# Query-key dots in float32r over the full array instead of float32 pairs on half arrays

## The reference

```
D_MODEL, SEQ, DEC_SEQ, PAST_LEN, DEPTH = 1024, 1024, 64, 256, 2
# group A: 8 query heads on 2 key heads, dim 64; indexer: 4 heads, dim 64, one key
q_a, k_a, v_a, gate_a, q_i, k_i, w_i, q_b, k_b, v_b, gate_b = split_cols(h @ w_in)
q_a, k_a, q_i, k_i = rope(...)
rel   = relu(einsum('bqhd,bsd->bqhs', q_i, k_i))            # index dots
score = einsum('bqhs,bqh->bqs', rel, w_i) * IDX_SCALE        # then the top 256 keys of each query
logits = einsum('bqngd,bqknd->bqngk', q_a, chosen_keys) * HD ** -0.5     # attention dots
o_a = softmax(logits) @ chosen_values
o_b = retention(rope(q_b), rope(k_b), v_b, state)            # 4 heads, dim 128
mixed = concat(o_a * silu(gate_a), groupnorm(o_b) * silu(gate_b))
x = x + gate * rms_norm(mixed @ w_out)
```

## Time and profile before

| what | value |
|---|---|
| median of three runs | 1437.32 us |
| span of the profiled execution, first to last instruction | 1434.8 us |
| what the median has beyond that span | 2.5 us |
| mean granted clock of TensorE | 0.996 |
| TensorE busy | 1389.2 us (97%) |
| VectorE busy | 1008.5 us (70%) |
| ScalarE busy | 784.4 us (55%) |
| GpSimd busy | 405.2 us (28%) |
| layer 0: `idx` steps | 38.8 to 116.4 us |
| layer 0: `ret` and `gate` steps | to 421.5 us |
| layer 0: `att` steps | to 610.7 us |
| layer 0: `out` steps | to 747.2 us |
| layer 1: `att` steps | 1106.2 to 1295.2 us |

### The profile page before, as it was taken

How to read it: one execution, slowest core, us unless ns; L and a number is a source line. 1 busy time by engine, 2 the same in 40 slices (tenths; PEclk the granted TensorE clock), 3 DMA queues, 4 the chain that set the end, 5 groups by cost and what they waited for, 6 DMA issues and landing times.

```text
span 1434.8 us, 24595 instructions
## 1 busy us (share of the span) xinstructions
PE 1389.2 (97%) x7687; PEld 1065.3 (74%) x7687; DVE 1008.5 (70%) x2983; ACT 784.4 (55%) x1916; POOL 405.2 (28%) x382
## 2 busy tenths in 40 slices
PE   6999999999999999999998999999999999999997
PEld 2865777888887677668877577878888766766886
DVE  0687889999996545542398789999999654555225
ACT  2555666666326665664454566666632566666432
POOL 3741333443331011001287124443343100100100
PEclk9999999999999999999999999999999999999999
DMA  9743333302232112213252111211223211222325
GB/s 314 232 135 100 94 122 110 83 23 60 58 90 66 43 39 69 81 65 105 88 181 69 41 32 44 59 40 43 62 58 90 66 34 46 69 65 67 112 74 176
DMA packets 125190, 122.05 MB, mean 85 GB/s; under 512 B 33256, under 2 KB 94024, under 8 KB 125064
## 3 DMA queue, kind: packets, MB, share of 16 engines
q1 hardware_dynamic: 124608, 120.36, 27.7%
q10 hardware_dynamic: 456, 0.13, 0.0%
HBM read 93.55 MB, written 26.90 MB: 84 GB/s over the span
## 4 chain that ended last, share of the span: by engine, by line
PE 57%; DVE 31%; issue 5%; POOL 3%; DMA 2%; ACT 2%; DVEq 0%; ACTq 0%; SPq 0%; POOLq 0%
DVE U L1787 11%; PE proj L1016 10%; PE proj L1017 10%; PE proj L1019 9%; PE turn L995 9%; PE logit L1043 7%; PE out_bank L1070 5%; PE spare L1043 2%; DVE turned L1742 2%; DVE by_cos_sin L1727 2%; DVE by_cos_sin L1725 2%; DVE probsT_more L1860 2%; DVE probsT_more L1864 1%; POOL h_lo L1565 1%; PE spare L981 1%
## 5 line engine op out<-in xcount | busy, mean ns | idle before, releaser
L1016 PE MATMUL proj<-w_hi,h_hi 128*128 128x512 f32 (+2 forms) x1440 | 574.6, 399 | 0.8 <-POOL h_lo L1565 0.4
L1017 PE MATMUL proj<-w_lo,h_hi 128*128 128x512 f32 (+2 forms) x1440 | 535.5, 372 | 0.0
L1019 PE MATMUL proj<-w_hi,h_lo 128*128 128x512 f32 (+2 forms) x1280 | 477.7, 373 | 0.0
L1559 POOL TENSOR_TENSOR w_lo<-w_raw,w_hi 128x512 fp32r<-128x512 f32 (+2 forms) x160 | 202.4, 1266 | 745.6 <-ACT w_hi L1265 745.4
L1016 PEld LDWEIGHTS proj<-w_hi,h_hi 128*128 128x128 f32 x1440 | 272.1, 189 | 50.7 <-issue 15.1
L1017 PEld LDWEIGHTS proj<-w_lo,h_hi 128*128 128x128 f32 x1440 | 272.3, 189 | 31.0
L1019 PEld LDWEIGHTS proj<-w_hi,h_lo 128*128 128x128 f32 x1280 | 240.5, 188 | 37.1
L1787 DVE TENSOR_SCALAR_CACHE_REDUCE U<-score,cand 128x384 bf16<-128x384 f32 x310 | 223.0, 752 | 2.2
L1043 PE MATMUL logit<-keys,queries 64*128 64x512 f32 (+4 forms) x454 | 137.2, 542 | 2.3 <-ACT U L1408 1.6
L1388 ACT ACTIVATE probsT_more<-turn 128x512 f32<-128x512 f32 (+3 forms) x156 | 76.1, 491 | 95.8 <-PE turn L995 95.6
L995 PEld LDWEIGHTS turn<-ident,U 128*128 128x128 f32 x584 | 65.9, 140 | 52.1 <-issue 37.0
(11 more groups left out here) (206 smaller groups left out, 2131.8 us busy)
## 6 DMA issues: line engine op xcount, KB each, us to landing
w_raw<-in_w_in_dram SPq DMA_DIRECT2D x80, 256.0 KB, 3.2
probsT_more<-in_w_ada_dram SPq DMA_DIRECT2D x64, 256.0 KB, 3.7
score<-mixed_dram SPq DMA_DIRECT2D x36, 256.0 KB, 3.0
score<-in_w_ada_dram SPq DMA_DIRECT2D x32, 256.0 KB, 5.0
w_raw<-in_w_out_dram SPq DMA_DIRECT2D x32, 256.0 KB, 3.4
U<-in_x_prompt_dram SPq DMA_DIRECT2D x12, 512.0 KB, 4.1
mixed_dram<-U SPq DMA_DIRECT2D x24, 192.0 KB, 2.1
gates_dram<-U SPq DMA_DIRECT2D x18, 256.0 KB, 2.0
```

The lines of the kernel that those rows point to most:

```text
L1016: nc.tensor.matmul(out, h_hi[:, k, tile], hi, start=(k == 0), stop=False)
L1017: ins = nc.tensor.matmul(out, h_hi[:, k, tile], lo, start=False, stop=(t == SAMPLE and k == KT - 1))
L1019: ins = nc.tensor.matmul(out, h_lo[:, k, tile], hi, start=False, stop=(k == KT - 1))
L1559: nc.gpsimd.tensor_tensor(w_lo[:, s % WS, 0:w], w_raw[:, n % RAWS, 0:w], w_hi[:, s % WS, 0:w].bitcast(F32), ALU.subtract).then_inc(w_lo_re ...
```

## The change

Queries and keys get the same treatment as the projections' operands. `keys` becomes `keys_hi` and `keys_lo`. `queries` holds for each head its high part on one half of the partitions and its low part on the other half. Two float32r matmuls over all 128 partitions, against `keys_hi` and `keys_lo` (the key stands on both halves), then give a head's dots. ScalarE writes the high parts, VectorE subtracts to get the low parts, and it is VectorE's subtraction that frees the bank. The weights have 14 slots instead of 16, and slices 6 and 7 of the next chunk are split in the sample's step, once its first quarter is multiplied.

```diff
--- before.py
+++ after.py
@@ -304,6 +304,17 @@
     return (C + 1) * KT + t if t < KT and C + 1 < DEPTH * NCH else None
 
 
+def early_slice(g):
+
+    return weight_slice(g) if 0 <= g < STEPS and g % NT < KT - LATE else None
+
+
+def late_slices(g):
+
+    return [weight_slice(g - n) for n in range(LATE, 0, -1)] \
+        if 0 <= g < STEPS and g % NT == SAMPLE and g // NT + 1 < DEPTH * NCH else []
+
+
 def raw_items():
 
     out = [("w", s) for s in range(KT)]
@@ -361,7 +372,8 @@
 RAWS = 3
 RELUS = 4
 ADA_SLOTS = 5
-WS = 2 * KT
+WS = 2 * KT - 2
+LATE = 2 * KT - WS
 ADAS = 8
 
 
@@ -479,8 +491,9 @@
         w_hi = sb("w_hi", [P, WS, 512], F32R)
         w_lo = sb("w_lo", [P, WS, 512], F32R)
         w_raw = sb("w_raw", [P, RAWS, 512])
-        keys = sb("keys", [P, NKEYS])
-        queries = sb("queries", [P, 2, GROUP // 2, P])
+        keys_hi = sb("keys_hi", [P, NKEYS], F32R)
+        keys_lo = sb("keys_lo", [P, NKEYS], F32R)
+        queries = sb("queries", [P, 2, GROUP, P], F32R)
         probs_last = sb("probs_last", [P, 1024])
         probsT_more = sb("probsT_more", [P, 3072])
         score = sb("score", [P, SCORE_COLS])
@@ -624,6 +637,9 @@
         index_weights_ready = sem("index_weights_ready")
         turn_full = [sem(f"turn_full{n}") for n in range(RB)]
         turn_taken = [sem(f"turn_taken{n}") for n in range(RB)]
+        high_turned = sem("high_turned")
+        high_cached = sem("high_cached")
+        first_quarter = sem("first_quarter")
         idx_turned = sem("idx_turned")
         idx_turn_taken = sem("idx_turn_taken")
         logit_full = [sem(f"logit_full{n}") for n in range(RB)]
@@ -1017,6 +1033,8 @@
                     ins = nc.tensor.matmul(out, h_hi[:, k, tile], lo, start=False, stop=(t == SAMPLE and k == KT - 1))
                     if t < SAMPLE:
                         ins = nc.tensor.matmul(out, h_lo[:, k, tile], hi, start=False, stop=(k == KT - 1))
+                if quarter == 0 and t == SAMPLE:
+                    ins.then_inc(first_quarter, 1)
                 if quarter == QUARTERS - 1:
                     ins.then_inc(proj_done, 1)
 
@@ -1038,10 +1056,11 @@
                     ring.wait_free(pe, ("l", g, h, p))
                 for h, p in heads:
                     a, m = parts[p]
-                    rows_ = slice(HD * (h % 2), HD * (h % 2) + HD)
                     key = ("l", g, h, p)
-                    ring.filled(nc.tensor.matmul(ring.bank(key)[:, 0:m], queries[rows_, HILO[g] % 2, h // 2, :],
-                                                   keys[rows_, k0 + a:k0 + a + m], start=True, stop=True), key)
+                    out, both_halves = ring.bank(key)[:, 0:m], queries[:, HILO[g] % 2, h, :]
+                    nc.tensor.matmul(out, both_halves, keys_hi[:, k0 + a:k0 + a + m], start=True, stop=False)
+                    ring.filled(nc.tensor.matmul(out, both_halves, keys_lo[:, k0 + a:k0 + a + m],
+                                                 start=False, stop=True), key)
 
             def turn_probs(n, final):
 
@@ -1260,7 +1279,9 @@
                 C = s // KT
                 w = WIDTH[C % NCH]
                 act.wait_ge(raw_landed[n % RAWS], raw_value(n))
-                if C >= 2:
+                if s % KT >= KT - LATE and C:
+                    act.wait_ge(first_quarter, C)
+                elif C >= 2:
                     act.wait_ge(proj_done, (C - 1) * NT)
                 nc.scalar.activation(w_hi[:, s % WS, 0:w], w_raw[:, n % RAWS, 0:w], ACT.Copy).then_inc(w_hi_ready, 1)
 
@@ -1365,8 +1386,11 @@
                 t = lct(g)[2]
                 blk = t if t < SAMPLE else SAMPLE_BLOCK
                 wait_keys_free(act, g)
-                nc.scalar.activation(queries[:, HILO[g] % 2], src[:, 0:256].rearrange("p (h n) -> p h n", n=P), ACT.Copy)
-                ring.take(nc.scalar.activation(keys[:, blk * P:(blk + 1) * P], src[:, 256:384], ACT.Copy), ("q", g))
+                for half in (0, 1):
+                    at = slice(HD * half, HD * half + HD)
+                    nc.scalar.activation(queries[at, HILO[g] % 2, half::2, :],
+                                         src[at, 0:256].rearrange("p (h n) -> p h n", n=P), ACT.Copy)
+                nc.scalar.activation(keys_hi[:, blk * P:(blk + 1) * P], src[:, 256:384], ACT.Copy).then_inc(high_turned, 1)
 
             def take_cache(g):
                 turns.wait_full(act, ("cache", g))
@@ -1374,8 +1398,8 @@
                     j = HILO_STEPS[HILO[g] - NT + 1]
                     n = valid_keys(SAMPLE) if kind(j) == "idx" else blocks_of(SAMPLE)[1] * P
                     ring_of(j).wait_full(act, ("l", j, 3, len(key_parts(n)) - 1))
-                turns.take(nc.scalar.activation(keys[:, SAMPLE_KEYS:SAMPLE_KEYS + PAST],
-                                                turns.bank(("cache", g))[:, 0:PAST], ACT.Copy), ("cache", g))
+                nc.scalar.activation(keys_hi[:, SAMPLE_KEYS:SAMPLE_KEYS + PAST],
+                                     turns.bank(("cache", g))[:, 0:PAST], ACT.Copy).then_inc(high_cached, 1)
 
             def take_probs(n):
                 g, h = head(n)
@@ -1483,10 +1507,12 @@
             for i in range(-1, STEPS + 2):
                 if i < 0:
                     split_hidden(0, 1)
-                if i + 1 < STEPS:
-                    if weight_slice(i + 1) is not None:
-                        split_weights(weight_slice(i + 1))
+                if early_slice(i + 1) is not None:
+                    split_weights(early_slice(i + 1))
                 for q in range(QUARTERS):
+                    if q == 2:
+                        for s in late_slices(i + 1):
+                            split_weights(s)
                     if q == 0:
                         late(i - 2)
                         if 0 <= i < STEPS and tested_bit(i) is not None:
@@ -1646,8 +1672,10 @@
                     input_diagonal(*raw_rows(i))
                 if i < 0:
                     lower_hidden(0, 1)
-                if i + 1 < STEPS and weight_slice(i + 1) is not None:
-                    lower_weights(weight_slice(i + 1))
+                if early_slice(i + 1) is not None:
+                    lower_weights(early_slice(i + 1))
+                for s in late_slices(i + 1):
+                    lower_weights(s)
                 for l, t in hidden_turns(i - 1):
                     if l == 0 and i >= 0:
                         lower_hidden(l, t)
@@ -1741,6 +1769,28 @@
                                                ALU.add))
                 signal(nc.vector.tensor_tensor(turned[:, ro % 2, 0:w], by_cos[:, 0:w], by_sin[:, 0:w], ALU.add),
                        rope_done, ro + 1)
+
+            def lower_turned(g):
+
+                ring, t = turns_of(g), lct(g)[2]
+                blk = t if t < SAMPLE else SAMPLE_BLOCK
+                at = slice(blk * P, (blk + 1) * P)
+                src = ring.bank(("q", g))
+                dve.wait_ge(high_turned, HILO[g] + 1)
+                for half in (0, 1):
+                    have, other = (slice(HD * h, HD * h + HD) for h in (half, 1 - half))
+                    do(nc.vector.tensor_tensor(queries[other, HILO[g] % 2, half::2, :],
+                                               src[have, 0:256].rearrange("p (h n) -> p h n", n=P),
+                                               queries[have, HILO[g] % 2, half::2, :].bitcast(F32), ALU.subtract))
+                take(ring, nc.vector.tensor_tensor(keys_lo[:, at], src[:, 256:384], keys_hi[:, at].bitcast(F32),
+                                                   ALU.subtract), ("q", g))
+
+            def lower_cache(g):
+
+                at = slice(SAMPLE_KEYS, SAMPLE_KEYS + PAST)
+                dve.wait_ge(high_cached, sum(1 for k in range(g + 1) if has_cache_turn(k)))
+                take(turns, nc.vector.tensor_tensor(keys_lo[:, at], turns.bank(("cache", g))[:, 0:PAST],
+                                                    keys_hi[:, at].bitcast(F32), ALU.subtract), ("cache", g))
 
             def weigh_relus(g, q):
 
@@ -2122,6 +2172,10 @@
                         finish_attention(att_step(i, q, BACK_SLOT))
                     if q == 2 and kind(i - 2) == "ret":
                         measure_retained(i - 2)
+                    if q == TURN_QUARTER and kind(i) in ("idx", "att"):
+                        lower_turned(i)
+                    if q == TURN_QUARTER and has_cache_turn(i):
+                        lower_cache(i)
                 if mixed_turn(i):
                     lower_mixed(*mixed_turn(i))
                 if kind(i) == "idx":
```

## The result

The changed kernel takes **1449.74 us** (median of 4, 1446.47 to 1452.3) beside 1437.27 us of the kernel before (1436.86 to 1438.34): 1.0085 times, 95% interval 1.0071 to 1.0099. It is 12.5 us slower where 16.9 us faster was forecast. The profiled execution has a span of 1450.5 us against 1434.8, so 15.7 us are to be found in it; it is the slowest of the four, 2.6 us above their median, and so shows more than the 12.5 us.

A forecast was written before the change was run, and what follows sets the result against it. TensorE, busy 97% of the span, was taken as the bound. Terms -27.2 - 6.5 + 1 + 6 + 6.6 + 2 + 1.2 = -16.9 us took 1437.3 to 1420.4 us; own range 1410 to 1431, full range 1407 to 1439.

The forecast's parts named there:

- The price of the dots: Two heads' dots over 512 keys fall from 1.22 to 0.92 us; 128-column records take 0.11 us.
- 27.2 + 12.9 us: TensorE's savings from cheaper dots: 27.2 us in attention, 12.9 us in the index, of which only 6.5 was counted.
- The late slices: Splits moved into the sample's step cost 2 us at retention boundaries and 1.2 us between the layers.
- The start of attention: VectorE waits for ScalarE's copies without cover, delaying the mask and next rotation: 6 us over two layers.
- Narrow tiles: In attention's narrow tiles, copies and subtractions against TensorE's projection quarters are a draw: 1 us in all.
- In attention 36 x 1.1 = 40 us go into 331 us of stage with over 40% idle: hidden, as long as the order holds: VectorE's added subtractions in attention, 40 us, fit its idle time and cost nothing if the order holds.
- ScalarE's longer copies: One more copy in each index and attention step, up to 0.39 us, hidden in attention where ScalarE is 64% busy.
- TensorE has at least two projection quarters, 2 x 1.05 us, before it asks: In attention, TensorE's lead against about 1.1 us of copies and 1.1 of subtractions after the transposes.
- the sign that it named for its failure: TensorE waiting for VectorE's low parts in most attention steps, or slow narrow records, would show the prediction failed.
- the index steps: Where VectorE is full or hands over directly, 12 steps lose 0.55 us each, half of 0 to 1.1: 6.6 us.
- the handover sets the pace in attention: Rival: TensorE waits in each of 36 attention steps for bank or low parts, 0.8 us each: 1449 us, chance 0.10.
- The lower end of the full range, 1407 us: Fast end of the whole kernel's full range, 1407 to 1439 us; the forecast's own range began at 1410.

The follow-up runs named there:

- e1: Kernel before with only the dots changed to two whole-array float32r matmuls a head, without subtractions (products not the reference's): 1403.23 us.
- e2: Kernel before, float32 dots kept, with only the 14 weight slots and the two late slices taken over: 1438.45 us.
- e8: Changed kernel with VectorE's subtractions behind quarter 3's row maxima, only in attention steps that turn no mixed rows: 1441.04 us.
- e5: Changed kernel, but in attention steps ScalarE also copies the raw transposes to SBUF and GpSimd subtracts there: 1454.46 us.
- e3: Changed kernel with the dots back as float32 pairs over the high parts, low parts computed but unused: 1481.97 us.
- e13: e8 plus GpSimd making low parts in mixed-row steps, and layer 1's hidden-row index steps making them before weighing quarter 2's relus: 1432.74 us.
- e4: Changed kernel with subtractions behind quarter 3's row maxima in attention and index steps, except steps with mixed rows: 1454.54 us.
- e9: e8 with index steps' subtractions ahead of weighing quarter 2's relus and, unintended, the cache's low part at quarter 2 again: 1452.0 us.
- e11: e8 with GpSimd making the late slices' low parts in index chunks only after VectorE has made the sample's low parts: 1452.98 us.

## Why the prediction was wrong

**Right, by its own steps.** The price of the dots, wide and narrow (0.92 us a 512 group, 0.11 us for 128 columns, the way in gone). Gross it forecast 27.2 + 12.9 us; e1's stages give 23.0 in attention and 10.0 in the index, 33.0, which is 18% less. e1 also shows that four whole-array float32r passes beat two pairs of float32 ones side by side. The Trainium skill, "TensorE: Matmul & The Clock Gate", section "Why this matters for your kernels", advises the side by side form for short contractions. Against float32 pairs this measurement decides for the whole array, but it changed the type and the arrangement at once: float32r pairs on half arrays, with three products a head as in the projections, weren't run. The late slices: 3.2 us forecast, 2.1 in e2's span, but elsewhere: 2 us were put on the retention, and 1.9 of what came is in layer 1's index stage. The start of attention: 6 us forecast, 6.8 measured, with 1.1 of the clock in it. Narrow tiles: 1 us forecast, none measured. VectorE: 59 us more forecast, 63.6 measured.

**The step that failed** is "In attention 36 x 1.1 = 40 us go into 331 us of stage with over 40% idle: hidden, as long as the order holds" (the two stretches of 166 us make 332; that changes nothing). The work did fit, but idle time over a stage isn't idle time at the moment that counts. In the wide steps (two parts, exponentials of 768 columns, mixed rows) the chain transposes, exponential, copies, subtractions, maxima, exponential, transposes closes on itself, and 24.1 us were lost there, where the sum had nothing; 4.5 of them went to the clock in the second last step of each layer's attention. ScalarE's longer copies, which the prediction let hide as well, stand in the same chain. The margin "TensorE has at least two projection quarters, 2 x 1.05 us, before it asks" was worked out for the dots' wait alone; the bank's next user and the maxima behind the subtractions ask sooner. The prediction had named both, and priced neither. So the sign that it named for its failure, waits for VectorE's low parts in most attention steps, didn't show either: TensorE has 8 of them in 36 steps.

**Second, by size,** the index steps: 12 x 0.55 = 6.6 us forecast. The table gives 5.8 + 12.1 = 17.9 from e1 to the changed kernel, of which e2 had 0.1 + 1.9 alone: about 16 us. Three things the even split of 0 to 1.1 us had missed: a step of layer 1 in which VectorE takes hidden rows and weighs relus first (gap of 3.38 us), the collision with GpSimd, and the clock. What each of them cost isn't separated.

**The sum with measured terms,** on the span: -33.0 + 6.8 + 24.1 + 15.9 + 2.0 = +15.8 us; the spans differ by 15.7. The terms are differences between the stages of e1, e2 and the changed kernel, so that they add up says nothing more; what they show is where the time lies.

**The rival that came** is "the handover sets the pace in attention". Its mechanism is right, its spread isn't: not 0.8 us in each of 36 steps but nothing in 22 of them and 1 to 5 us in most of the others. That its 1449 us is the measured time is luck: it reckoned with 28.8 us in attention on top of the prediction's other terms, which had 6.6 us for the index stages where 16 came, and knew nothing of the clock. The lower end of the full range, 1407 us, has no sum behind it. A chance of 0.10 looks small for a change that puts a third engine into each handover.

**Open.** How much of each wide step's loss is the bank and how much the late maxima isn't separated: e8 moved the one, e5 the other, each with side effects. These comparisons also have the clock's share in them, which differs from one execution to the next.

## What to carry to other kernels

Idle share of a stage says that work fits, not that it hides: for a subtraction that stands between a producer's copy and a bank's release, walk one widest step with start times, and ask what each engine does at that moment and who else needs the bank. A handover through three engines in a row should be as short as it can be made; 1.3 us less of it a step, 0.9 on VectorE and 0.4 on ScalarE, was worth 28 us here, the clock's part included, and moving the subtraction to an idle but slower engine was worth less than nothing. Time the gain alone and the cost alone first: two runs (e1, e3) bounded the whole question. And before a few microseconds are put down to an edit, look at the granted clock: one stretch at half clock more or less is 1.6 us.

## What the hardware showed that I had not expected

**Short gaps can cost twice.** TensorE's clock, granted at 2.4 GHz nearly throughout before, fell to 1.2 GHz nine times in the changed kernel, the last microseconds left out. Stretches around the first attention dots (PE busy, ..., clock in the last but two columns):

```profile
434.00:438.20 4.20, 2.56 (x16) 2.24 (x15) 3.92 (x12) 0.72 (x1) 0.50 (x1) 1.00 0.00 0
438.30:441.70 3.40, 3.15 (x12) 3.15 (x13) 1.80 (x13) 2.20 (x9) 0.00 (x0) 0.53 0.26 58
441.80:446.00 4.20, 4.20 (x28) 4.13 (x27) 3.82 (x13) 2.49 (x10) 1.14 (x1) 0.99 0.37 98
```

TensorE had nine gaps of 1.92 us or more there, and each of the nine stretches began within 1.5 us of the end of one; the gaps up to 1.83 us had none behind them in this kernel. It is no border: e1 had a gap of 2.17 us and e13 one of 2.48 without a fall, and e3 a fall behind one of 1.74.

The runs take the clock apart from the gap. The second last step of attention has the same gap, 2.03 to 2.05 us, in the changed kernel, e4, e8, e9 and e11. It lasts 16.5 us where no fall follows (e8 in both layers, e4 and e11 in layer 1), 18.1 with a stretch of 3.4 us (e9 in both layers, the changed kernel, e4 and e11 in layer 0) and 19.4 with one of 6.8 (the changed kernel in layer 1). One stretch costs 1.6 us there, a double one 2.9. The changed kernel has 27 us more at half clock than the one before, eight such stretches, by this rate an estimated 12 us. Its four executions give less: two at a mean granted clock of 0.986 took 1452.3 and 1451.39 us, one at 0.993 took 1446.47, so 5.8 us for 20 us at half clock, and an estimated 8 us for the 27. So 8 to 12 of the 15.7 us of the profiled execution are an estimate of the clock's share; they are contained in the stage sums above. Even the execution at 0.993 was 9 us slower than the kernel before.

**An instruction of VectorE can wait for one of GpSimd.** VectorE's 0.42 us became 1.35 and its 0.62 became 1.46 while GpSimd worked on SBUF, and both were back at 0.42 and 0.62 in e11, where GpSimd stood still. GpSimd's own two took 1.33 us each, as its mean for that form (1320 ns in e8); so here only VectorE was held up.
